# Expert-choice routing on one Trainium2 core: the prompt's top-256 lists taken from four pieces on 64 partitions instead of two on 32

## The reference

```python
def ec_moe(x, w_router, w_gate, w_up, w_down):
    N = B * L                                   # 2048 (prompt) or 256 (sample)
    cap = max(1, EC_CAPACITY * N // N_EXPERTS)  # 256 or 32
    xt = x.reshape(N, D)
    aff = jax.nn.softmax((xt @ w_router).astype(jnp.float32), axis=-1)
    gates, idx = lax.top_k(aff.T, cap)
    xs = xt[idx]
    h = jax.nn.silu(jnp.einsum('ecd,edf->ecf', xs, w_gate)) * jnp.einsum('ecd,edf->ecf', xs, w_up)
    y = jnp.einsum('ecf,efd->ecd', h, w_down) * gates[..., None].astype(x.dtype)
    out = jnp.zeros((N, D), x.dtype).at[idx.reshape(-1)].add(y.reshape(-1, D).astype(x.dtype))
```

## Time and profile before

| | us |
|---|---|
| median of 3 runs (2938.06 to 2942.07) | 2941.3 |
| profiled execution, its own time | 2940.52 |
| its span, first to last instruction | 2938.5 |
| TensorE busy | 2579.2 (88%) |
| VectorE busy | 1912.9 (65%) |
| ScalarE busy | 1660.0 (56%) |
| GpSimd busy | 1055.4 (36%) |

### The profile page before, as it was taken

One profiled execution on the slowest core, in us unless ns is written; L12 is line 12 of the kernel. 1 busy time (PEld: TensorE's weight loads), 2 busy tenths in 40 slices (PEclk: granted clock), 3 DMA queues, 4 the chain that ended last, 5 costly groups with the idle time before them and its releaser, 6 DMA issues. The chain is left out here.

```text
span 2938.5 us, 45637 instructions
## 1 busy us (share of the span) xinstructions
PE 2579.2 (88%) x16813; PEld 1444.9 (49%) x16813; DVE 1912.9 (65%) x2737; ACT 1660.0 (56%) x2708; POOL 1055.4 (36%) x984
## 2 busy tenths in 40 slices
PE   7899999859999999978989896999502999999998
PEld 4455555425555555543332332555302666666664
DVE  5455555458888888868979895444396454545552
ACT  6634444349999999978548554333321454545440
POOL 1221211148888888867009101212020112222221
PEclk9999999969999999989999997999755999999999
DMA  7423333335211101136978795544511667666762
GB/s 185 117 60 90 88 103 84 85 74 186 75 37 35 28 21 37 38 87 250 307 245 273 271 313 171 161 146 140 182 57 39 185 223 235 194 193 204 233 179 33
DMA packets 268924, 415.99 MB, mean 142 GB/s; under 512 B 55390, under 2 KB 148958, under 8 KB 267168
## 3 DMA queue, kind: packets, MB, share of 16 engines
q1 hardware_dynamic: 219696, 344.39, 36.1%
q0 software_dynamic: 10752, 37.75, 5.5%
q10 hardware_dynamic: 38288, 31.37, 3.8%
HBM read 280.56 MB, written 132.86 MB: 141 GB/s over the span
## 5 line engine op out<-in xcount | busy, mean ns | idle before, releaser
L1162 POOL TENSOR_TENSOR at_p<-at_pf,at_p 128x512 f16<-128x512 f32 x424 | 510.8, 1214 | 136.3 <-ACT at_p L1296 109.6
L1424 DVE TENSOR_REDUCE at_mxs<-at_pM 128x1 f32<-128x512 f32 x512 | 342.2, 684 | 72.4 <-PE at_pM L1323 62.0
L1295 ACT ACTIVATE at_pf<-at_pS,at_scale 128x512 f32<-128x512 f32 x520 | 359.4, 691 | 28.0 <-PE at_pS L1348 27.2
L1296 ACT ACTIVATE at_p<-at_pS,at_scale 128x512 f16<-128x512 f32 x520 | 356.7, 686 | 0.0
L1367 PEld LDWEIGHTS at_pO<-at_vv,at_p 128*128 128x128 f16 x4160 | 233.4, 97 | 140.5 <-POOL at_p L1162 31.9
L1367 PE MATMUL at_pO<-at_vv,at_p 128*128 128x129 f16 x4160 | 267.4, 207 | 8.4 <-POOL at_p L1162 6.5
L3007 PE MATMUL ex_pY<-mo_down,ex_hT 128*128 128x512 f32 x512 | 224.0, 595 | 0.0
L1323 PE MATMUL at_pM<-at_k,at_q 96*128 96x512 f16 x512 | 189.5, 389 | 28.1 <-DVE at_q L1410 17.5
L1346 PE MATMUL at_pS<-at_q,at_k 97*128 97x512 f16 (+1 forms) x528 | 199.7, 378 | 3.9 <-issue 2.2
L1347 PE MATMUL at_pS<-at_q,at_k 96*128 96x512 f16 (+1 forms) x528 | 199.5, 378 | 0.0
L1348 PE MATMUL at_pS<-at_q,at_k 96*128 96x512 f16 (+1 forms) x528 | 198.4, 376 | 0.0
(11 more groups left out here) (351 smaller groups left out, 5911.0 us busy)
## 6 DMA issues: line engine op xcount, KB each, us to landing
sp_rows<-s_F SPq DMA_DIRECT2D x76, 512.0 KB, 5.5
s_F<-fs_a SPq DMA_DIRECT2D x72, 512.0 KB, 3.1
mo_raw<-in_w_gate SPq DMA_DIRECT2D x32, 1024.0 KB, 7.5
mo_raw<-in_w_up SPq DMA_DIRECT2D x32, 1024.0 KB, 7.5
mo_down<-in_w_down SPq DMA_DIRECT2D x16, 2048.0 KB
s_G<-sp_gg SPq DMA_DIRECT2D x72, 256.0 KB, 4.1
sp_tab<-tab_spec SPq DMA_DIRECT2D x76, 224.0 KB, 3.9
s_QK<-pj_R ACTq DMA_DIRECT2D x18, 768.0 KB, 4.7
```

The lines of the kernel that those rows point to most:

```text
L1162: eng.tensor_tensor(p2[r][:, :], pf[:, r, :], p1[r][:, :], ALU.subtract).then_inc(own_done if n in own else others_done, 1)
L1295: act.activation(pf[:, n % 4, :], pS[n % 2][:, 0:QB], ACT.Exp, scale=scale[:, 0:1])
L1296: act.activation(p1[n % 4][:, :], pS[n % 2][:, 0:QB], ACT.Exp, scale=scale[:, 0:1]).then_inc(pS_free, 1)
L1424: dve.tensor_reduce(mxs[:, j // NC, j % NC:j % NC + 1], pM[j % 2][:, :], AX.X, ALU.max).then_inc(pM_free, 1)
```

## The change

The prompt's 2048 tokens are split in four pieces of 512 in place of two of 1024. `aff` has 64 partitions: for the prompt, partitions 0 to 15 hold piece 0, 16 to 31 piece 2, 32 to 47 piece 1 and 48 to 63 piece 3. The sample stays in two halves of 128, each held twice. A list still has 256 entries per piece, in 32 rounds.

The pieces' lists are then joined in two steps. In the first, VectorE brings the lists of partitions 32 to 63 down to partitions 0 to 31, reversed (`later`), and keeps the larger of each two entries, with its token number. What comes out is 256 entries for each half of the prompt, but no longer in order: it falls and rises at most once. A network of eight steps puts it in falling order: step n compares entries that are 128, 64, ..., 1 apart and puts the larger one first, and among equal values the lower token number. A step is 11 VectorE instructions on 32 partitions. The second joining is the one that was there before, on slots turned to partitions; the sample's list is already whole by then and needs only two of its four transposes.

```diff
-    assert CAPS[0] == 2 * P
-    NC, NJ = len(SLOT_TILES), NT // 2
+    NC, NJ = len(SLOT_TILES), NTP // 4 + 1
-    tile_pairs = [(j, j + NTP // 2) for j in range(NTP // 2)] + [(NTP, NTP + 1)]
+    PIECE = (GROUPS[0] // 4, GROUPS[1] // 2)
+    tile_quads = [tuple(j + NTP // 4 * p for p in (0, 2, 1, 3)) for j in range(NTP // 4)] + [(NTP, NTP, NTP + 1, NTP + 1)]
+    R = 2 * E_N
...
-        ex = sb("ex", [P, NJ, 2, E_N])
-        top, tot, inv = sb("top", [P, NJ, 2]), sb("tot", [P, NJ, 2]), sb("inv", [P, NJ, 2])
-        aff = sb("aff", [2 * E_N, NJ * P])
-        idx = sb("idx", [2 * E_N, NTOK], U32)
+        ex = sb("ex", [P, NJ, 4, E_N])
+        top, tot, inv = sb("top", [P, NJ, 4]), sb("tot", [P, NJ, 4]), sb("inv", [P, NJ, 4])
+        aff = sb("aff", [4 * E_N, NJ * P])
+        idx = sb("idx", [4 * E_N, NTOK], U32)
+        listing, later = sb("listing", [4 * E_N, 2, NTOK]), sb("later", [R, 2, NTOK])
+        pairs = [sb(f"pairs{b}", [R, 2, NTOK]) for b in range(2)]
+        wins, ties, shift = sb("wins", [R, NTOK]), sb("ties", [R, CAPS[0] // 2]), sb("shift", [R, NTOK])
+        sooner = sb("sooner", [R, CAPS[0] // 2])
...
-            for j, pair in enumerate(tile_pairs):
-                for half, t in enumerate(pair):
-                    last = pe.transpose(pT[:, j, half, :], lg[:, t * P:(t + 1) * P], eye[0:E_N, 0:E_N])
+            for j, quad in enumerate(tile_quads):
+                for q, t in enumerate(quad):
+                    last = pe.transpose(pT[:, j, q, :], lg[:, t * P:(t + 1) * P], eye[0:E_N, 0:E_N])
...
-            pe.wait_ge(listed, 4)
+            pe.wait_ge(listed, 2)
             for c in range(NC):
-                for m in range(4):
+                for m in range(4 if c < 2 else 2):
...
-            act.activation(aff[:, HALF[0]:], pA[:, HALF[0]:NJ * P], ACT.Copy).then_inc(aff_ready, 1)
-            act.activation(aff[:, 0:HALF[0]], pA[:, 0:HALF[0]], ACT.Copy).then_inc(aff_ready, 1)
+            act.activation(aff[:, PIECE[0]:], pA[:, PIECE[0]:NJ * P], ACT.Copy).then_inc(aff_ready, 1)
+            act.activation(aff[:, 0:PIECE[0]], pA[:, 0:PIECE[0]], ACT.Copy).then_inc(aff_ready, 1)
...
-                rest = aff[:, sum(HALF[:g]):sum(HALF[:g + 1])]
+                rest = aff[:, sum(PIECE[:g]):sum(PIECE[:g + 1])]
...
-                    v8, i8 = lists[:, 1, eight], idx[:, eight]
+                    v8, i8 = listing[:, 1, eight], idx[:, eight]
...
-            step(dve.tensor_copy(lists[:, 0, 0:NTOK], idx[:, :]), listed, 1)
+            step(dve.tensor_copy(listing[:, 0, :], idx[:, :]), paired, 1)
+            for g in range(2):
+                at = slice(sum(CAPS[:g]), sum(CAPS[:g + 1]))
+                dve.tensor_scalar(later[:, 0, at], listing[R:, 0, at][:, ::-1], float(PIECE[g]), None, ALU.add).then_inc(paired, 1)
+                dve.tensor_copy(later[:, 1, at], listing[R:, 1, at][:, ::-1]).then_inc(paired, 1)
+            dve.wait_ge(paired, 5)
+            soon, late = listing[0:R], later
+            step(dve.tensor_tensor(wins[:, :], soon[:, 1, :], late[:, 1, :], ALU.is_ge), paired, 6)
+            step(dve.tensor_tensor(shift[:, :], soon[:, 0, :], late[:, 0, :], ALU.subtract), paired, 7)
+            step(dve.tensor_tensor(shift[:, :], shift[:, :], wins[:, :], ALU.mult), paired, 8)
+            step(dve.tensor_tensor(pairs[0][:, 1, :], soon[:, 1, :], late[:, 1, :], ALU.max), paired, 9)
+            step(dve.tensor_tensor(pairs[0][:, 0, :], late[:, 0, :], shift[:, :], ALU.add), paired, 10)
             of_sample = slice(CAPS[0], NTOK)
             for m in range(2):
-                ins = dve.tensor_copy(lists[:, m, NTOK:].rearrange("p (j n) -> p j n", j=PARTS - 1),
-                                      lists[:, m, of_sample].unsqueeze(1).to_broadcast([2 * E_N, PARTS - 1, CAPS[1]]))
+                ins = dve.tensor_copy(lists[:, m, CAPS[0]:].rearrange("p (j n) -> p j n", j=PARTS),
+                                      pairs[0][:, m, of_sample].unsqueeze(1).to_broadcast([R, PARTS, CAPS[1]]))
             ins.then_inc(listed, 1)
+            count, half = 10, CAPS[0] // 2
+            apart_by = [half >> n for n in range(half.bit_length())]
+            for n, d in enumerate(apart_by):
+                def sides(x, m):
+                    view = x[:, m, 0:CAPS[0]].rearrange("p (k s d) -> p k s d", s=2, d=d)
+                    return view[:, :, 0, :], view[:, :, 1, :]
+                out = lists if d == 1 else pairs[(n + 1) % 2]
+                (i0, i1), (v0, v1) = sides(pairs[n % 2], 0), sides(pairs[n % 2], 1)
+                (to_i0, to_i1), (to_v0, to_v1) = sides(out, 0), sides(out, 1)
+                win, tie, first_of, by = (x[:, 0:half].rearrange("p (k d) -> p k d", d=d) for x in (wins, ties, sooner, shift))
+                dve.tensor_tensor(win, v0, v1, ALU.is_gt).then_inc(paired, 1)
+                dve.tensor_tensor(tie, v0, v1, ALU.is_equal).then_inc(paired, 1)
+                dve.tensor_tensor(first_of, i0, i1, ALU.is_lt).then_inc(paired, 1)
+                dve.tensor_tensor(by, i0, i1, ALU.subtract).then_inc(paired, 1)
+                dve.wait_ge(paired, count + 3)
+                dve.tensor_tensor(tie, tie, first_of, ALU.mult).then_inc(paired, 1)
+                dve.tensor_tensor(to_v0, v0, v1, ALU.max).then_inc(paired, 1)
+                dve.tensor_tensor(to_v1, v0, v1, ALU.min).then_inc(paired, 1)
+                dve.wait_ge(paired, count + 5)
+                dve.tensor_tensor(win, win, tie, ALU.add).then_inc(paired, 1)
+                dve.wait_ge(paired, count + 8)
+                dve.tensor_tensor(by, by, win, ALU.mult).then_inc(paired, 1)
+                dve.wait_ge(paired, count + 9)
+                dve.tensor_tensor(to_i0, i1, by, ALU.add).then_inc(paired, 1)
+                dve.tensor_tensor(to_i1, i0, by, ALU.subtract).then_inc(paired, 1)
+                count += 11
+                dve.wait_ge(paired, count)
             for m in range(2):
-                dve.tensor_copy(lists[:, 2 + m, 0:CAPS[0]], lists[:, m, 0:CAPS[0]][:, ::-1])
-                for j in range(PARTS):
-                    at = CAPS[0] + j * CAPS[1]
-                    ins = dve.tensor_copy(lists[:, 2 + m, at:at + CAPS[1]], lists[:, m, of_sample][:, ::-1])
-                ins.then_inc(listed, 1)
+                ins = dve.tensor_copy(lists[:, 2 + m, 0:CAPS[0]], lists[:, m, 0:CAPS[0]][:, ::-1])
+            ins.then_inc(listed, 1)
             dve.wait_ge(cols_ready, NC)
-            first, second = cols[:, 0:2, :, 0, :], cols[:, 2:4, :, 1, :]
+            first, second = cols[:, 0:2, 0:2, 0, :], cols[:, 2:4, 0:2, 1, :]
+            sample = cols[:, 0:2, 2, 0, :]
+            gates = chosen["gate"]
             step(dve.tensor_tensor(better[:, :, :], first[:, 1], second[:, 1], ALU.is_ge), merged, 1)
-            step(dve.tensor_tensor(chosen["gate"][:, :, :], first[:, 1], second[:, 1], ALU.max), merged, 2)
-            for c, (g, a, n) in enumerate(SLOT_TILES):
-                step(dve.tensor_scalar(token[:, c, :], second[:, 0, c], float(HALF[g]), None, ALU.add), merged, 3 + c)
-            step(dve.tensor_tensor(apart[:, :, :], first[:, 0], token[:, :, :], ALU.subtract), merged, NC + 3)
-            step(dve.tensor_tensor(apart[:, :, :], apart[:, :, :], better[:, :, :], ALU.mult), merged, NC + 4)
-            step(dve.tensor_tensor(token[:, :, :], token[:, :, :], apart[:, :, :], ALU.add), merged, NC + 5)
+            step(dve.tensor_tensor(gates[:, 0:2, :], first[:, 1], second[:, 1], ALU.max), merged, 2)
+            step(dve.tensor_scalar(token[:, 0:2, :], second[:, 0], float(HALF[0]), None, ALU.add), merged, 3)
+            step(dve.tensor_tensor(apart[:, :, :], first[:, 0], token[:, 0:2, :], ALU.subtract), merged, 4)
+            step(dve.tensor_tensor(apart[:, :, :], apart[:, :, :], better[:, :, :], ALU.mult), merged, 5)
+            step(dve.tensor_tensor(token[:, 0:2, :], token[:, 0:2, :], apart[:, :, :], ALU.add), merged, 6)
+            step(dve.tensor_copy(token[:, 2, :], sample[:, 0]), merged, 7)
+            step(dve.tensor_copy(gates[:, 2, :], sample[:, 1]), merged, 8)
```

More of the change, by code:

```diff
@@ L2613, in choose @@
 def choose(nc, io, chosen, weights):
-    assert CAPS[0] == 2 * P
-    NC, NJ = len(SLOT_TILES), NT // 2
+    assert CAPS[0] == 2 * P and CAPS[0] <= GROUPS[0] // 4
+    NC, NJ = len(SLOT_TILES), NTP // 4 + 1
     HALF = tuple(n // 2 for n in GROUPS)
-    tile_pairs = [(j, j + NTP // 2) for j in range(NTP // 2)] + [(NTP, NTP + 1)]
-    assert len(tile_pairs) == NJ
+    PIECE = (GROUPS[0] // 4, GROUPS[1] // 2)
+    tile_quads = [tuple(j + NTP // 4 * p for p in (0, 2, 1, 3)) for j in range(NTP // 4)] + [(NTP, NTP, NTP + 1, NTP + 1)]
+    assert len(tile_quads) == NJ and sum(PIECE) == NJ * P
+    R = 2 * E_N
     with ExitStack() as ctx:
```

13 lines of the change are left out of this document (7 added, 6 removed).

## The result

| | before | after |
|---|---|---|
| median of 4 runs, us | 2941.7 (2938.1 to 2944.1) | 2914.4 (2912.4 to 2917.1) |
| ratio, 95% interval | | 0.991 [0.9898, 0.9922] |
| span of the profiled execution, us | 2938.5 | 2915.0 |
| VectorE busy, us | 1912.9 | 1885.7 |

The kernel is faster by 27.3 us, 0.9%, and the interval of the ratio leaves out 1. The forecast was 2912.6 us; the measured median lies inside the stated range.

The account below looks back on a forecast made before the run. VectorE's serial listing alone was taken to end the routing stage; terms -51.2, -0.5, +3.2, +20.9 and -1.1 summed to -28.7 us, giving 2912.6 us after a 0.8 us adjustment to the median, range 2907.5 to 2921.5 us.

Parts of the forecast that it names:

- rounds: VectorE's 32 search rounds over the prompt, at 512 columns instead of 1024, each save 1.601 us: -51.2 us.
- front: Ahead of the search: logit transposes, transposes back and steps over 320 columns for 288 change slightly: -0.5 us.
- first joining: Moving the lists down and keeping the larger of each two entries, four moves and five two-operand instructions: +3.2 us.
- network: Eight ordering steps of eleven VectorE instructions, three waited for in full, at 2.62 us a step: +20.9 us.
- tail: Behind the ordering: fewer reversing copies and list transposes, and a changed last merge: -1.1 us.
- stage: The routing part, which lists each expert's tokens before the experts start; claimed shorter by 28.7 us.
- low and high ends: Range of the forecast total: 2907.5 us with no network waits and good clock, 2921.5 us with rivals and spread.
- a microsecond taken from the listing is one taken from the total: VectorE alone delays the experts, where TensorE runs without a gap, so listing time saved shortens the whole kernel equally.
- No overlap: Rival: every ordering instruction costs 0.325 us, waited for or not; +7.7 us, total 2920.3 us; chance 0.09.
- Strides: Rival: interleaved operands in later ordering steps cost double per column; +7.4 us, or +2.1 us in two steps; chance 0.10.
- Slower, by passes over partitions: Rival: search instructions on 64 partitions run as two passes of 32, saving nothing there; total 2963.8 us; chance 0.03.
- The clock: TensorE's clock may fall to its lower level in the first expert, once, twice or not: 1.4 us either way.

Follow-up runs that it names:

- prices: Changed kernel plus 36 idle, individually waited VectorE instructions (additions and `max` on 32 to 128 partitions) behind the ordering network; 2938.0 us in one run.
- eight pieces: Changed kernel with its network instructions reordered, then split into eight pieces of 256 tokens on 128 partitions, with two networks; 2908.3 us, ratio 0.9882.

## Why the prediction was right

By its own terms, each read from the profile after:

| term | predicted | measured |
|---|---|---|
| rounds | -51.2 | -50.7 (128.32 to 77.61) |
| front | -0.5 | -0.45 (7.48 to 7.03) |
| first joining | +3.2 | +3.0 (3.70 from 2197.09 to 2200.79, for 0.66 before) |
| network | +20.9 | +20.4 (2200.79 to 2221.20) |
| tail | -1.1 | -1.0 (6.14 from 2221.20, for 7.16 before) |
| stage | -28.7 | -28.7 |

- **The sum.** It is met to 0.1 us, closer than its two large terms: 0.5 us too much saving in the rounds and 0.5 us too much cost in the network cancel. That part is luck. The items listed for the tail add up to -1.0 us and were entered as -1.1; the low and high ends add up to 2907.3 and 2921.3 us where 2907.5 and 2921.5 are stated.
- **The bound.** VectorE alone ends the stage, before and after, and leaving the network out showed it for a stage of 95 us too. The step "a microsecond taken from the listing is one taken from the total" holds: the rest of the span is 687.4 to 687.9 us in seven of the nine profiles of changed kernels and 687.9 to 688.8 us in the four of the kernel before, at stages from 95 to 144 us; an expert takes 41.40 us in both kernels. The first gather began 22.4 us earlier (2228.45 for 2250.89 us) and not 28.7, because of the 6.3 us ahead of the stage.
- **The rounds.** The line through 128 and 1024 columns was right; what it missed is 4 ns an instruction for the second group of 32 partitions, some 0.5 us in all. That `max` costs nearly the same on 64 partitions as on 32 was taken from another operation; the prices run is what shows it (682 and 686 ns).
- **The network.** The count of waits was right, three full ones of eleven. The durations came from rows of 128 partitions and are 272 to 279 ns on 32 instead of 290; spacings are 0.20 and 0.31 us instead of 0.205 and 0.325. The step takes 2.55 us, 2.62 forecast.
- **No overlap** (0.09): excluded by the profile after, and priced by a run, +7.2 us where I had +7.7. The Trainium skill (VectorE: DVE Perf Modes) has two sections on it: by The DRAIN you can't avoid the time would have been 2920.3 us, an estimate; Two Vector instructions with no wait between them, by which only a held instruction waits for all earlier ones, agrees with the starts 0.20 us apart of instructions of 0.27 us.
- **Strides** (0.10): excluded; the last two steps take what the first does.
- **Slower, by passes over partitions** (0.03): excluded; a round takes 2.29 us, and 3.17 would have decided for it.
- **The clock.** The forecast allowed 1.4 us either way for the first expert. The same 24 matmuls take 3.11 us in nine profiles (two of the kernel before, seven of changed kernels), 4.41 and 4.79 us in the other two of the kernel before, and 5.94 us in prices and eight pieces. Against the 4.79 us that is 1.7 us less or 1.2 more, so the size was about right; in the first pair it fell to the good side, which was luck. No run shows whether the change has a part in which of them comes. What I had not allowed for is that the time ahead of the stage moves by 4 to 5 us between executions of one kernel: the first pair of profiles shows a gain of 23.5 us where the stage gives 28.7.

The median came out 1.8 us above the forecast, and none of that is the stage's: 0.4 us of it is the fourth run of the kernel before, which moved its median from 2941.3 to 2941.7 us. The forecast took the code ahead of the listing as equal in both kernels. The profiles bear this out to within some 2 us and the timed runs to within 0.7 us in the mean, and the cause of that shift stays open.

## What to carry to other kernels

Where one engine's chain of short dependent instructions ends a stage, count its full waits and its unwaited starts apart and take both spacings from rows: that gave the length of 88 new instructions within 3%. Splitting a list so that more partitions work saves columns by halves (rounds -50.7 us, then -24.7) while the joining costs nearly the same at each level (23.4 us, then 20.8 with the network reordered), so find the level at which the two meet before building it. Where a wait would otherwise hold the engine, independent instructions put between dependent ones take that time (2.3 us saved here), and a stage's own length between two fixed instructions resolves tenths of a microsecond where whole times resolve five.

## What the runs showed of the hardware that I had not expected

- VectorE's price grows a little with partitions: 4 ns for each further 32, for an addition over 128 columns (279 to 292 ns) and for `max` over 512 (682 to 695 ns). In the unwaited networks it cannot be seen: 273 ns on 32 and on 64 partitions.
- An instruction behind a wait that holds it is itself 6 ns longer in the trace (278 against 272 ns); behind a wait that is already met it takes 272 ns (lines 2814 and 2818).
- The short value load ahead of `max_index` and `match_replace` takes 79 ns on 32 partitions, 83 on 64 and 92 on 128.
- Behind the listing TensorE's granted clock (0.50) comes back to 1.00 at different points of the first expert, in two profiles of the kernel before ahead of its first 24 matmuls (3.11 us) and in the third one within them (4.41 us); in the first one it came back ahead of them and fell to 0.50 once more within them (4.79 us). Over all kernels these matmuls took 3.11 to 5.94 us.
- Code that no edit touched takes 432 to 435 us for the same 1440 matmuls, and the stage behind it began anywhere between 2102.1 and 2112.5 us in thirteen profiles.
